# Rows added in two float32r parts instead of three bf16 parts, second weights as one 8192-byte piece per partition, even and odd units in the column tiles

## What is computed

```python
def swiglu(x, w1, w3, w2):
    return (jax.nn.silu(x @ w1) * (x @ w3)) @ w2
...
    def expert_block(args):
        toks, e, wts = args
        out = swiglu(xpad[toks], w1[e], w3[e], w2[e])
        return out * wts[:, None].astype(out.dtype)
...
    routed = jax.ops.segment_sum(y.reshape(n_slots, D), slot_tok, num_segments=T + 1)[:T]
    shared = swiglu(xf, ws1, ws3, ws2)
    return (routed + shared).reshape(B, S, D)
```

## Time and profile before

| | |
|---|---|
| median of 3 runs | 2237.6 us (2233.91 to 2243.11) |
| profiled execution, its own time | 2242.32 us |
| its span, first to last instruction | 2240.6 us |
| TensorE (PE) busy | 2132.4 us, 95% of the span |
| VectorE (DVE) busy | 973.5 us, 43% |
| ScalarE (ACT) busy | 510.0 us, 23% |
| moved by DMA | 599.13 MB, mean 267 GB/s |
| granted TensorE clock, mean | 0.985 of full speed |

### The profile page before, as it was taken

One profiled execution on the slowest core, in us unless ns is written; L12 is line 12 of the kernel. 1 busy time (PEld: TensorE's weight loads), 2 busy tenths in 40 slices (PEclk: granted clock), 3 DMA queues, 4 the chain that ended last, 5 costly groups with the idle time before them and its releaser, 6 DMA issues. The chain is left out here.

```text
span 2240.6 us, 34873 instructions
## 1 busy us (share of the span) xinstructions
PE 2132.4 (95%) x13404; PEld 1232.9 (55%) x13404; DVE 973.5 (43%) x2062; ACT 510.0 (23%) x1077; POOL 59.7 (3%) x143
## 2 busy tenths in 40 slices
PE   5999999899999999979999988999999999799998
PEld 3844444556556565557454445556565565367475
DVE  2673423544444444428634244444444443353153
ACT  2223112122222222223231111222222222113131
POOL 1000002000000000000000030000000000100000
PEclk9999999999999999989999999999999999899999
DMA  9652838699999999845527437999999998531721
GB/s 325 203 206 75 300 113 319 224 385 376 385 378 382 386 379 381 341 179 179 198 105 260 167 130 279 380 382 381 383 378 389 377 386 286 178 111 57 225 69 56
DMA packets 165286, 599.13 MB, mean 267 GB/s; under 512 B 13052, under 2 KB 17760, under 8 KB 130656
## 3 DMA queue, kind: packets, MB, share of 16 engines
q1 hardware_dynamic: 163808, 595.10, 70.7%
q0 software_dynamic: 1408, 3.10, 0.7%
HBM read 597.11 MB, written 1.05 MB: 267 GB/s over the span
## 5 line engine op out<-in xcount | busy, mean ns | idle before, releaser
L1198 PE MATMUL banks<-weight_ring,h_t 128*64 128x256 f32 x4224 | 481.8, 381 | 3.2 <-DVE h_t L1950 3.2
L1198 PEld LDWEIGHTS banks<-weight_ring,h_t 128*64 128x64 f32 x4224 | 298.3, 137 | 174.0 <-issue 38.2
L849 PE MATMUL banks<-weight_ring,h_t 128*128 128x512 f32 x768 | 335.8, 593 | 4.1 <-issue 1.6
L849 PEld LDWEIGHTS banks<-weight_ring,h_t 128*128 128x128 f32 x768 | 145.1, 190 | 187.6 <-issue 182.8
L1976 DVE SCALAR_TENSOR_TENSOR conv_t<-banks,slot_weight,xn 128x512 f32<-128x512 f32 x132 | 99.1, 751 | 293.5 <-ACT xn L1503 293.5
L1186 PEld LDWEIGHTS banks<-z,sp_ 128*128 128x128 bf16 x3168 | 178.8, 98 | 55.8 <-issue 49.3
L1186 PE MATMUL banks<-z,sp_ 128*128 128x128 bf16 x3168 | 201.0, 220 | 4.9 <-DVEq L1940 4.9
L1238 PE MATMUL banks<-xn,conv 128*128 128x512 bf16 x792 | 185.9, 385 | 6.7 <-issue 4.0
L1503 ACT ACTIVATE xn<-banks,slot_weight 128x512 bf16<-128x512 f32 x132 | 90.7, 687 | 342.6 <-PE banks L1225 342.6
L1956 DVE TENSOR_TENSOR z<-banks,z 128x128 f32<-128x128 f32 x132 | 38.5, 292 | 230.0 <-ACT z L1488 230.0
L2209 PE MATMUL banks<-weight_ring,h_t 128*128 128x512 f32 (+2 forms) x384 | 134.1, 509 | 2.9 <-ACTq L2385 2.9
(11 more groups left out here) (467 smaller groups left out, 2045.2 us busy)
## 6 DMA issues: line engine op xcount, KB each, us to landing
weight_ring<-in_w SPq DMA_DIRECT2D x264, 1024.0 KB, 10.9
weight_ring<-in_w_in SPq DMA_DIRECT2D x36, 2048.0 KB, 11.5
slots<-in_w SPq DMA_DIRECT2D x68, 1024.0 KB, 8.5
weight_ring<-in_w_mod SPq DMA_DIRECT2D x24, 2048.0 KB, 10.0
qk<-in_w SPq DMA_DIRECT2D x32, 1024.0 KB, 7.0
z<-in_w SPq DMA_DIRECT2D x32, 1024.0 KB, 11.4
weight_ring<-in_w_out SPq DMA_DIRECT2D x8, 2048.0 KB, 7.8
weight_ring<-in_w_in SPq DMA_DIRECT2D x10, 1024.0 KB, 7.7
```

Source lines behind the costliest of these rows:

```text
L849: mm = nc.tensor.matmul(bank[:, 0:cols], stationary[:, k, t * P:(t + 1) * P], w[:, k, 0:cols], start=(k == 0), stop=(k == KT - 1))
L1198: mm = nc.tensor.matmul(h_bank[g * SLOTS:(g + 1) * SLOTS, 0:FF], x_blk[:, j // 2, k, own], w13(j)[:, :, k, g * (FF // 2):(g + 1) * (FF // 2)],
```

## The change

Four edits, made together:

- **Two parts.** `o_parts` holds two parts in float32r, a 4-byte type which TensorE takes in another way than float32: part 0 is written by ScalarE as before (now as float32r), part 1 is VectorE's rest, written as float32r at once. ScalarE's second rounding and VectorE's second subtraction are gone, and `o_rest_ready` and `o_second_ready` with them; `o_ready` follows VectorE's first operation and takes both meanings.
- **Adding.** `pair_add` makes 2 x 2 x 2 = 8 matmuls of float32r in place of 12 of bf16. Its stationary operand `slot_of` is float32r too, and has memory of its own at the place of `conv_t`.
- **w2 in one piece.** Partition p gets rows 2p and 2p + 1 of w2, 8192 bytes in one piece.
- **Even and odd units.** So that this layout fits, column tile g of `block_h` takes the units g, g + 2, g + 4, ...: the moving operand is read with a step of two elements.

```diff
-                sp.dma_start(w2_slots[s], A["w2"][ds(l, 1), ds(e, 1)].rearrange("a b (f p) n -> p (a b f) n", p=P))\
+                sp.dma_start(w2_slots[s].rearrange("p f n -> p (f n)"), A["w2"][ds(l, 1), ds(e, 1)].rearrange("a b (p f) n -> p (a b f n)", f=2))\
...
                             mm = nc.tensor.matmul(h_bank[g * SLOTS:(g + 1) * SLOTS, 0:FF], x_blk[:, j // 2, k, own],
-                                                  w13(j)[:, :, k, g * (FF // 2):(g + 1) * (FF // 2)],
+                                                  w13(j)[:, :, k, g::2],
...
                         pe.wait_ge(o_ready, nth(it, 2 * i + h))
                         for t in range(T):
-                            for c in range(PARTS):
+                            for c in range(HALVES):
                                 mm = nc.tensor.matmul(y_bank[t][h][:], slot_of[:, i % PAIRS, t * P:(t + 1) * P],
                                                       o_parts[:, c, h * CHUNK:(h + 1) * CHUNK],
                                                       start=False, stop=True, skip_group_check=True)
...
-                        pe.wait_ge(o_rest_ready, nth(it, b - 2))
+                        pe.wait_ge(o_ready, nth(it, b - 2))
...
-                    for h in range(2):
-                        col = slice(h * CHUNK, (h + 1) * CHUNK)
-                        act.wait_ge(o_rest_ready, nth(it, 2 * i + h))
-                        nc.scalar.activation(o_parts[:, 1, col], o_rest[:, col], ACT.Copy).then_inc(o_second_ready, 1)
...
-                        v.scalar_tensor_tensor(o_rest[:, col], o_banks[h][:], own, o_parts[:, 0, col], ALU.mult, ALU.subtract)\
-                            .then_inc(o_rest_ready, 1)
-                    for h in range(2):
-                        col = slice(h * CHUNK, (h + 1) * CHUNK)
-                        dve.wait_ge(o_second_ready, nth(it, 2 * i + h))
-                        v.tensor_tensor(o_parts[:, 2, col], o_rest[:, col], o_parts[:, 1, col], ALU.subtract).then_inc(o_ready, 1)
+                        v.scalar_tensor_tensor(o_parts[:, 1, col], o_banks[h][:], own, o_parts[:, 0, col].bitcast(F32), ALU.mult,
+                                               ALU.subtract).then_inc(o_ready, 1)
...
-        K.xn = keep("xn", [P, T, D])
+        with nc.sbuf_tensor("xn", [P, T, D], F32) as K.xn:
+            pass
+        K.o_parts = keep("o_parts", [P, HALVES, D], F32R)
```

More of the change, by code:

```diff
@@ L27 @@
 BF16 = mybir.dt.bfloat16
+F32R = mybir.dt.float32r
 ALU = mybir.AluOpType
@@ L58 @@
 PARTS = 3
+HALVES = 2
 MOD_CHUNKS = 6 * D // CHUNK
@@ L464, in first_block @@
         conv = sb("conv", [P, CT, SEQ])
-        conv_t = sb("conv_t", [P, CT, SEQ])
+        with nc.sbuf_tensor("conv_t", [P, CT, SEQ], F32) as conv_t:
+            pass
+        slot_of = sb("slot_of", [P, CT * SEQ // (T * P), T * P], F32R)
         conv_std = sb("conv_std", [P, SEQ])
@@ L549, in first_block @@
         turned = conv_flat[:, 0:PAIRS * 2 * P].rearrange("p (i b n) -> p i b n", i=PAIRS, b=2)
-        slot_of = conv_flat[:, 512:768].bitcast(BF16).rearrange("p (i n) -> p i n", i=PAIRS)
-        o_rest = conv_t[:].rearrange("p c n -> p (c n)")
-        o_parts = K.xn[:].rearrange("p t n -> p (t n)").bitcast(BF16)[:, 0:PARTS * D].rearrange("p (c n) -> p c n", c=PARTS)
+        o_parts = K.o_parts
         w2_slots = [slots2[:, 0], slots2[:, 1], qk[:].rearrange("p t n -> p (t n)").rearrange("p (f n) -> p f n", f=2),
@@ L610, in first_block @@
             sem(f"block_{n}") for n in ("h_done", "sigmoid_ready", "act_ready", "turn_done", "turned_ready"))
-        gather_done, x_ready, o_done, o_first_ready, o_rest_ready, o_second_ready, o_ready = (
-            sem(f"half_{n}") for n in ("gather_done", "x_ready", "o_done", "o_first_ready", "o_rest_ready",
-                                       "o_second_ready", "o_ready"))
+        gather_done, x_ready, o_done, o_first_ready, o_ready = (
+            sem(f"half_{n}") for n in ("gather_done", "x_ready", "o_done", "o_first_ready", "o_ready"))
         hot_ready, weight_ready, added = (sem(f"pair_{n}") for n in ("hot_ready", "weight_ready", "added"))
@@ L1279, in _ @@
                 with pe.If(no_second < 1):
-                    pe.wait_ge(o_rest_ready, nth(last_turn, 1))
+                    pe.wait_ge(o_ready, nth(last_turn, 1))
                     for half in range(2):
```

## The result

| | before | after |
|---|---|---|
| median | 2237.6 us | 2220.75 us (2215.22 to 2221.57) |
| profiled execution, its own time | 2242.32 us | 2220.96 us |
| its span | 2240.6 us | 2219.2 us |
| mean granted clock | 0.985 | 0.982 |

The ratio is 0.9915 with a 95% interval of 0.9892 to 0.9938: faster by 0.85%, a third of the 2.6% that was forecast, and just outside the range. Of the five runs of the change, the three at a mean granted clock of 0.982 took 2220.75 to 2221.57 us and the two at 0.985 took 2216.13 and 2215.22 us.

What follows compares the result with a forecast made beforehand. TensorE was taken to set the pair of 16.50 us, with the DMA following. 2242.3 - 55.2 + 3.2 - 4 - 1.7 = 2184.6 us profiled, 4.7 us above the median, so 2180 us; range 2168 to 2220 us.

Steps and rivals of the forecast that it cites:

- Even and odd units ... I take 0: In block_h: reading the moving operand with a step of two costs nothing, 0 us.
- The upper bound, 3.4 us a pair: In block_h: the step costs one cycle more a column; as a rival 225 us more, 2405 us, chance 0.03.
- The add: In pair_add: four fewer matmuls gain 0.862 us, 64 times, 55.2 us less; slower first loads cost 3.2 us more.
- I take the low bound: In pair_add: a float32r matmul of 512 columns is priced as bf16, 0.216 us, so 1.73 us an add.
- The two-cycle rival: In pair_add: float32r takes two cycles a column, 56 us more in the loops, 2292 us, slower; chance 0.12.
- The ends of the layers: At each MoE layer's last add: 4 us less in the first layer, 1.7 us less in the second.
- the rival had 15.5: In the expert loops: the DMA becomes the bound, with a floor of 15.5 us a pair; chance 0.10.
- ScalarE's and VectorE's removed work: In the pairs: the removed subtraction and rounding lie on no chain of TensorE's in full flow, so gain nothing.
- The merged semaphore: At block_turn(a): it comes no later, with 3.2 us of cover before TensorE gets there.
- pair_w2's cover of 0.3 us: Before pair_w2: after the shorter add, the next pair's rows are still ready 0.3 us before TensorE gets there.
- float32r as dear as float32: In pair_add: two records a matmul, 6.93 us an add, 275 us more, about 2455 us; chance 0.03.
- the three rivals that would make the kernel slower: In pair_add and block_h: two cycles a column 0.12, the step slowing block_h 0.03, float32r as dear as float32 0.03.

Runs made afterwards that it cites:

- run 1: The change with straight units and the old w2 layout, so only the float32r adds are left: 2196.08 us, ratio to before 0.9815.
- run 2: The change with straight units, but w2 still in one piece of 8192 bytes a partition: 2197.37 us, ratio to before 0.9812.
- run 3: The kernel before with only the step of two and w2 in one piece, the old add kept: 2264.51 us, ratio to before 1.0114.
- run 4: The change with block_h's moving operand read at a step of four instead of two: 2722.64 us in one run, with one pair more in the second layer.
- run 6: The change with straight units and the old w2 layout, each float32r matmul cut into two of 256 columns: 2193.29 us in one run.
- run 5: The kernel before with the add made of two of its three bf16 parts: 2185.52 us in one run.
- run 9: The change with straight units and the old w2 layout, the short branch at the layer's end written first: 2187.44 us, ratio to before 0.9772.
- run 7: The change with straight units and w2 in 4096-byte pieces, block_h over 7 of its 8 steps of k: 2132.43 us in one run.
- run 8: The change with straight units and w2 in 8192-byte pieces, block_h over 7 of its 8 steps of k: 2132.92 us in one run.
- run 10: The change with straight units and w2 in 4096-byte pieces, block_h over 6 of its 8 steps of k: 2120.40 us in one run.
- run 11: The change with straight units and w2 in 8192-byte pieces, block_h over 6 of its 8 steps of k: 2117.11 us in one run.

## Why the prediction was wrong

The forecast was a span shorter by 57.7 us, and it was 21.4. The 36.3 us between them, by its steps:

**"Even and odd units ... I take 0": the step that failed, 21.8 us.** The loss is 0.33 us a pair, 66 times. The reasoning was that float32 records ask for an element only at half the clock. That is no cover: they slow down by 0.33 / 32 = 0.010 us for each two side by side nevertheless (runs 1, 2 and 3). The prediction's own sign of being wrong on the step, block_h over 3.7 us, came: 3.73 and 3.77 us. The neighbour that I used, a weight load with a step of eight, reads another operand, and it did show 0.117 against 0.108 us; I called that hardly a cost. A few per cent of one short load are nothing, but block_h is 7.1 of 16.5 us, and 4.6% there are more than a third of the gain that was forecast (21.8 of 57.7 us). The upper bound, 3.4 us a pair, was put as a rival of 0.03 that is all or nothing; nothing in the range stood for a cost of 5%. It was not an upper bound of what a step can cost either: a step of four costs 14.74 - 7.17 = 7.57 us a pair (run 4).

**The add, 4.6 us.** Sized at 0.862 less 0.05 = 0.81 us a pair, it measured 0.74. "I take the low bound" was right as to mechanism: one record for each float32r matmul, and one column a cycle (runs 1, 6). The two-cycle rival falls: it needed 0.324 us a matmul or more, and records lie 0.24 apart. With it falls the figure of the Trainium skill (SBUF — State Buffer, "A bandwidth-pool intuition that's wrong"), about 614 GB/s for the moving operand, read as a limit in bytes as the prediction did: 512 columns of 128 x 4 bytes in 0.24 us are about 1090 GB/s. What I missed is a surcharge of about 0.02 us on each matmul (runs 5, 6), where the prediction had 0.05 us once an add; it is partly paid back by the shorter gap ahead of the add.

**The ends of the layers, 3.6 us.** Forecast 4 and 1.7, measured 0.6 and 1.5. In the earlier trace rows I took the named releaser, VectorE's L1981, for the cause. But the add's first half needs only the first of its two subtractions, which ended at about 968.55 (0.69 us after 967.86), 0.5 us before the add began; in run 3 it is 0.06. The engine had most likely been waiting for its own instructions as well (the q8 packet at 966.0 to 966.4, runs 3 and 9), and when the result came sooner only the name changed, to "issue" (2.96 us after, 2.69 before). The second layer's row had said so before the change. Run 9 shows what that wait cost run 1 at the two ends: 2.9 and 4.9 us. A small slip beside it: (5.30 - 0.4) / 11 in the second layer is 0.445 us, not 0.43.

**Outside the loops, 6.3 us.** Foreseen by no step. In the mixer between the layers as many instructions take TensorE longer; windows over it, before and then after:

```profile
973.60:1361.60 388.00, 359.85 (x1282) 198.62 (x1282) 181.11 (x354) 84.37 (x144) 17.52 (x10) 0.97 0.48 171
```

```profile
958.70:1352.60 393.90, 364.70 (x1282) 200.77 (x1282) 180.99 (x354) 84.56 (x144) 17.52 (x10) 0.96 0.47 170
```

4.85 of its 5.9 us are TensorE's busy time at a lower granted clock. Runs 1, 3, 5 and 9 have 392.7, 394.2, 391.5 and 391.6 us here, and none of runs 1 to 3 and 5 to 11 less than 390.2. Runs 3 and 5 share no edit, so it goes with no single one. Whether the one execution of before was lucky, or any shift of the MoE layer's end moves the clock in the mixer, stays open; the profiled execution of the change is one at 0.982, and those at 0.985 took 5 us less.

**What held.** TensorE sets the pair, and each pair moves by the sum of its instructions: 15.76, 15.64, 15.81 and 16.85 us came out as summed. The DMA was not the bound; its floor is 15.05 us where the rival had 15.5, 0.7 us under the pair without the step. The pieces of w2 are worth nothing here. ScalarE's and VectorE's removed work pays nothing by itself: run 5 keeps all of it and has the pair of 15.64 us. The merged semaphore shows no wait in the loops. pair_w2's cover of 0.3 us held in all runs: the only idle time ahead of it, 3.1 us in two waits for VectorE's h_t, is the same in every run and in the kernel before.

**Slips in the sums.** "float32r as dear as float32" was priced from the kernel before (275 us more) but added to the forecast; against the 1.73 us that the forecast took it is 64 x (6.93 - 1.73) = 333 us more, about 2513 us and not 2455. And the three rivals that would make the kernel slower have 0.12, 0.03 and 0.03, together 0.18, where "slower" was given 0.15. Neither touches the forecast.

## What to carry to other kernels

An edit on the operand of the largest matmul is costed in per cent of that matmul, not as free or ruinous: here 4.6% of block_h ate almost half of what the shorter add gave, and it paid for a layout that the profile already said nobody waits for. Where a wait's releaser ends just before the waiting instruction starts, look for another such place in the program: if one of them says "issue", removing the result's delay may gain little. The jump over the code of a branch that is not taken can cost microseconds (2.9 and 4.9 us here), so the likely case belongs first.

## What the runs showed of the hardware that was not expected

- A float32 moving operand read every second element lengthens the row of matmuls by 4.6%; every fourth element makes it 2.06 times as long (block_h, two column tiles side by side that take alternate elements).
- float32r goes at one column a cycle: 0.124 us for 256 columns and about 0.24 for 512, against 0.216 of bf16. Its weight loads show 188 to 192 ns each and yet come every 0.124 us: the record of a load doesn't say how often one can be had.
- The last add of a layer, behind a jump over an untaken branch, was preceded by 2.7 to 4.3 us of idle TensorE in the kernel before, the change and run 1, with a transfer of 0.02 MB on an instruction queue near the start of the idle time; the granted clock over that add was then 0.5 to 0.7. With the branches exchanged 0.45 us was left, for a result (run 9). That the transfer brings TensorE's own instructions fits these cases but no row shows it.
- Transfers of 1 MB reach 418 GB/s with w2 in pieces of 4096 bytes and 422 with 8192, each in a stretch where TensorE waits for them (runs 10 and 11, 500 to 600 us).
